# A causal mask as a product on TensorE in place of two selections on GpSimd: a macaron decoder layer with stick-breaking attention

## The chip, the cores and the metric

The kernel runs on one core of one Trainium2 chip. The metric is device microseconds (us) of one execution. The engines are TensorE (PE, with its weight loads PEld shown apart), VectorE (DVE), ScalarE (ACT), GpSimd (POOL) and SyncE (SP), which issues the transfers. Each runs its own list of instructions in order and they meet through semaphores.

## What is computed

One decoder layer on 1024 tokens of width 1024, all in float32: a SwiGLU block of inner width 2816, then a mixer block, then a second SwiGLU block, with RMS norms before each and at the end. The mixer has a pooling branch, an attention branch with 8 heads of 64, and gates. The attention branch is where the change lies. For query t and key s it computes

```python
z = (q . k) * scale
mask = kpos < qpos                                    # strictly causal
log_1m_beta = where(mask, log_sigmoid(-z), 0.0)
log_a = log_sigmoid(z) + reverse_cumsum(log_1m_beta) - log_1m_beta
a = where(mask, exp(log_a), 0.0)
out = a @ v
```

So a weight is sigmoid(z) times the product of 1 - sigmoid(z) over the keys between s and t. Where the mask is false the factor 1 - sigmoid is 1 and the weight is 0.

## The kernel before

Every float32 product is made of three products of fp32r operands (high by high, low by high, high by low), where fp32r is the type that the operands of these products have. All engines have lists written out by hand. The program runs through: norm and first SwiGLU, the combined input projection, the pooling branch, then the attention stage, the branch and output projections, the second SwiGLU and the last norm.

The attention stage works on 64 tiles, 8 heads by 8 query tiles of 128 rows; `TILE_ORDER` takes the query tiles of a head as 7, 6, 1, 0, 5, 4, 3, 2. A tile with query tile qt has (qt + 1) * 128 keys; up to 512 keys are one chunk, more are two, and the chunk that holds the diagonal comes first. There are 96 chunks. For each tile:

- PE, `logits`: q by k_hi, then q by k_lo, into one of three PSUM banks (L1334, L1336).
- ACT, `betas`: two sigmoids of the bank, 1 - beta into `keep` (L1811) and beta into `a` or `a2` (L1812); the second raises `sg_ok`.
- POOL, `mask_diagonal`: two `affine_select` on the last 128 columns of the tile, 1 into `keep` and 0 into `a` above the diagonal (L2626); each raises `masked`.
- DVE, `weigh_keys`: waits for `sg_ok` and `masked`, then a reversed scan of products over `keep` into `tail_p` (L2471), and `a` times `tail_p` (L2475, raises `a_ok`).
- PE, `turn`, two steps later: transposes the weights block by block with the identity `ident` (L1349).
- ACT, `turned_hi` (L1826), and DVE, `turned_lo` (L2484, raises `alo`): the high and low parts of what was turned.
- PE, `weigh`, once for two tiles: values by the turned weights (L1365 with the high part, L1366 with the low part).

Between these, PE runs the gates' products (L1188, `gate_parts`), 512 columns wide, in portions that `GATE_MARKS` sets for each step. They are independent of the attention and are there to fill the time in which PE would wait for a tile. After the stage the last gate products run (`GATE_TAIL`), then the branch projection (L1257).

POOL has little else in this stage: 16 products of a gate with the pooled branch (L2633).

At the program's start, POOL writes constants and the identity (L2610), and ACT, DVE and PE take the first norm, transposes and the first unit of the first SwiGLU (`up_units(0)`: a SiLU on ACT at L1496, then sums and low parts on DVE at L1905 and L1950 to L1999, then products on PE at L1047 and L1091).

Of the kernel before, what the change touches and what calls it, by code (L numbers as in the profile page):

```python
# [6 lines left out]
P = 128  # L7
# [96 lines left out]
TILES = attention_tiles()  # L104
NA = len(TILES)


CHUNKS = [sum(len(x["chunks"]) for x in TILES[:n]) for n in range(NA + 1)]
# [30 lines left out]
GATE_FIRST = [min(fb for fb, x in enumerate(GATE_BANKS) if x[0] == j) for j in range(KT)]  # L139
GATE_LAST = [max(fb for fb, x in enumerate(GATE_BANKS) if x[0] == j) for j in range(KT)]  # L140
PIECES = 4


def piece_start(j):
# [19 lines left out]
def macaron_layer(nc, x, ffn1_norm, ffn1_w_gate_up, ffn1_w_down, mix_norm, w_in, pool_w_group, pool_scale,  # L164
                  w_branch_pool, w_branch_attn, w_out, ffn2_norm, ffn2_w_gate_up, ffn2_w_down, final_norm, out):
    f32, f32r, i32 = mybir.dt.float32, mybir.dt.float32r, mybir.dt.int32
    ACT = mybir.ActivationFunctionType
    ALU = mybir.AluOpType
# [3 lines left out]
    with ctx:  # L172

        base = (nc.sbuf_base + 31) // 32 * 32
        K = 1024
# [5 lines left out]
        C0 = base + 200 * K  # L181
        G0 = C0 + 3200

        def at(name, shape, dt, offset):
            return nc.alloc_sbuf_tensor_at(name, shape, dt, offset=offset)
# [37 lines left out]
        for o0 in (120, 150):  # L223
            w = len(dn_slots)
# [58 lines left out]
        w_raw = at("w_raw", [P, 2, 2, KT, P], f32, R0)  # L283

        ident = at("ident", [P, P], f32, C0)
        o = C0 + 2560
        pos_i = at("pos_i", [P, PAD], i32, o)
        pos_f = at("pos_f", [P, PAD], f32, o + 64)
# [16 lines left out]
        zeros_f = at("zeros_f", [P, P], f32, base + 194 * K)  # L305
# [21 lines left out]
        keep = at("keep", [P, 2, SEQ], f32, X0 + 16384)  # L327
        a = at("a", [P, 2, SEQ], f32, X0 + 24576)
        a2 = at("a2", [P, SEQ], f32, o + 36864)
# [35 lines left out]
        def sem(name):  # L365
            return ctx.enter_context(nc.semaphore(name))
# [96 lines left out]
        gate_free = [sem(f"gate_free{b}") for b in range(2)]  # L463
        z_ok = sem("z_ok")
        sg_ok = sem("sg_ok")
        masked = sem("masked")
        scan_ok = sem("scan_ok")
        a_ok = sem("a_ok")
        t_ok = sem("t_ok")
# [534 lines left out]
        def _(pe):  # L1004
# [317 lines left out]
            def logits(n, part):  # L1322

                x_ = TILES[n]
                slot, qs = x_["head"] % 2, slice(x_["qt"] * P, (x_["qt"] + 1) * P)
                c, (c0, c1) = CHUNKS[n] + part, x_["chunks"][part]
                if n % NT == 0 and part == 0:
                    pe.wait_ge(head_in[slot], 96 * (x_["head"] // 2 + 1))
                if c in (0, 1):
                    wait_bank(2 + c, Q_GATE)  # L1330
                if c >= 3:
                    pe.wait_ge(sg_ok, c - 2)
                b, w = 2 + c % 3, c1 - c0
                nc.tensor.matmul(bank[:, b, 0:w], q_st[:, slot, qs], k_hi2[:, slot, c0:c1], start=True, stop=False,  # L1334
                                 skip_group_check=True)
                last = nc.tensor.matmul(bank[:, b, 0:w], q_st[:, slot, qs], k_lo2[:, slot, c0:c1], start=False,  # L1336
                                        stop=True, skip_group_check=True)
                last.then_inc(z_ok, 1)
# [33 lines left out]
            for s in range(NA + DRAIN):  # L1372
# [10 lines left out]
                if s < NA:  # L1383
                    n = len(TILES[s]["chunks"])
# [33 lines left out]
        def _(act):  # L1418
# [142 lines left out]
            def up_units(which):  # L1561

                even, odd, units = which, 1 - which, UNITS // 2 * which
                if which:
                    for i in range(2):
                        act.wait_ge(act_sp[i], 16 * units)
                plain_silu(which, 0, 0)
                plain_hi(which, 1, odd, units + 1)
                sums_of_u_hi(which, 0)
                sums_of_u_hi(which, 1)  # L1570
                plain_silu(which, 0, 1)
                sums_of_u_hi(which, 2)
                weights_hi(which, 2, even, units + 2)
                sums_of_u_hi(which, 3)
                sums_hi(which, 2, even)
                plain_silu(which, 1, 0)
                plain_silu(which, 1, 1)
                with act.Fori(1, UNITS // 2 - 1) as i:
                    up_unit(which, 2 * i, 0, units + i, more=(odd, units + i + 1))
                    up_unit(which, 2 * i + 1, 1, units + i, more=(even, units + i + 2))  # L1580
                n = UNITS - 2
                up_unit(which, n, 0, units + n // 2, more=(odd, units + n // 2 + 1))
                first_part(which, n + 1, 1, units + n // 2)
                dn_hi_of(2 * which, 0)
                silu(which, n + 1, 1, 0)
                second_part(which, n + 1, 1)
                dn_hi_of(2 * which, 1)
                silu(which, n + 1, 1, 1)
# [71 lines left out]
            def split_static(gg):  # L1660
                split_hi(gg, gg % 2, None if gg < 2 else quad_of(gg - 2))

            up_units(0)
            down(0, 2)

# [233 lines left out]
        def _(dve):  # L1899
# [564 lines left out]
            def weigh_keys(n):  # L2464

                w = TILES[n]["width"]
                dve.wait_ge(sg_ok, CHUNKS[n + 1])
                dve.wait_ge(masked, 2 * n + 2)
                if n:
                    dve.wait_ge(a_ok, n)  # L2470
                nc.vector.tensor_tensor_scan(tail_p[:, 0:w][:, ::-1], keep[:, n % 2, 0:w][:, ::-1],  # L2471
                                             zero_col[:, :].to_broadcast([P, w]), 1.0, ALU.mult, ALU.add).then_inc(scan_ok, 1)
                dve.wait_ge(scan_ok, n + 1)
                b = weights_of(n)[:, 0:w - 1]
                nc.vector.tensor_tensor(b, b, tail_p[:, 1:w], ALU.mult).then_inc(a_ok, 1)  # L2475
# [109 lines left out]
        @block.gpsimd  # L2585
        def _(pool):
            def norm_rows(k):

                for pos in range(NT):
                    t, n = pos, NT * k + pos  # L2590
                    pool.wait_ge(ms_ok, n + 1)
                    if k == 3 and t >= 4:
                        pool.wait_ge(part_ok, t - 3)
                        nc.gpsimd.tensor_scalar(mean_eps[:, k, t:t + 1], mean_sq[:, k, t:t + 1], part_sq[:, t:t + 1], EPS,
                                                ALU.add, ALU.add).then_inc(eps_ok, 1)
                    else:
                        nc.gpsimd.tensor_scalar(mean_eps[:, k, t:t + 1], mean_sq[:, k, t:t + 1], EPS, None,
                                                ALU.add).then_inc(eps_ok, 1)
                    pool.wait_ge(eps_ok, n + 1)
                    if n == 0:  # L2600
                        pool.wait_ge(half_set, 1)
                    nc.gpsimd.tensor_tensor(rstd[:, k, t:t + 1], mean_eps[:, k, t:t + 1], minus_half[:, :],
                                            ALU.pow).then_inc(rstd_ok, 1)

            nc.gpsimd.iota(pos_i[:, :], pattern=[[1, PAD]], base=1, channel_multiplier=0).then_inc(pos_set, 1)
            nc.gpsimd.memset(minus_half[:, :], -0.5).then_inc(half_set, 1)
            nc.gpsimd.memset(zeros_f[:, :], 0.0).then_inc(const_set, 1)
            nc.gpsimd.memset(zero_col[:, :], 0.0).then_inc(const_set, 1)
            pool.wait_ge(const_set, 2)
            nc.gpsimd.affine_select(out=ident[:, :], in_=zeros_f[:, :], compare_op=ALU.not_equal, fill=1.0, base=0,  # L2610
                                    pattern=[[-1, P]], channel_multiplier=1).then_inc(const_set, 1)
            norm_rows(0)
            norm_rows(1)

            pool.wait_ge(dn_ok, TAKEN)
            nc.gpsimd.memset(xpad[:, :, 0:PAD], 0.0).then_inc(const_set, 1)

            def weights_of(n):
                return a2[:, :] if n % 3 == 2 else a[:, n % 3, :]

            def mask_diagonal(n):

                w = TILES[n]["width"]
                pool.wait_ge(sg_ok, CHUNKS[n] + 1)
                for dst, fill in ((keep[:, n % 2, w - P:w], 1.0), (weights_of(n)[:, w - P:w], 0.0)):
                    nc.gpsimd.affine_select(out=dst, in_=dst, compare_op=ALU.is_gt, fill=fill, base=0,  # L2626
                                            pattern=[[-1, P]], channel_multiplier=1).then_inc(masked, 1)

            def gate_pool(i):

                pool.wait_ge(y_in[i % 2], 16 * (i // 2 + 1))
                pool.wait_ge(gate_free[0], i + 1)
                nc.gpsimd.tensor_tensor(gst[:, 0, :], gst[:, 0, :], pool_y[:, i % 2, :], ALU.mult).then_inc(gated, 1)  # L2633

            for s in range(NA + DRAIN):
                if s < NA:
                    mask_diagonal(s)
                for fb in BANKS_DONE[s]:
                    if fb % 2 == 0:
                        gate_pool(fb // 2)  # L2640
            norm_rows(2)
            norm_rows(3)
# [26 lines left out]
```

## Time and profile before

| | |
|---|---|
| median of 3 runs | 1937.92 us (1937.5 to 1938.38) |
| span of the profiled execution | 1937.1 us |
| PE busy | 1923.7 us, 99% |
| DVE / ACT / POOL busy | 69% / 40% / 7% |
| attention stage, 883 to 1156 us | 273.0 us, PE busy 270.76 |

The profile is of one execution; its span lies 0.8 us under the median of the runs, which is what the runs count around the span. Durations below are from that execution. A matmul's printed duration runs from its start to its modelled end, so it is longer than the distance to the next one: the distance of two starts is what a matmul costs PE.

### The profile page before, as it was taken

The numbers are of one execution on the slowest core, as the hardware profiler recorded it, in microseconds if no ns is written. First come the engines' busy times: TensorE is split into PE (matmuls) and PEld (weight loads), VectorE is DVE, ScalarE is ACT, GpSimd is POOL, SyncE is SP. The second block draws the span as 40 slices with busy tenths as digits, with TensorE's granted clock in tenths as the row PEclk, the third lists the DMA queues.
The fourth block names the chain that finished last, engine by engine and source line by source line (L and its number), as shares of the span: only waits on it lengthen the run. The fifth ranks groups of instructions, "written<-read, shape, count | busy, mean of one in ns | idle before, by whom it ended". The sixth has DMA issues, their size and how long they took to land.

```text
span 1937.1 us, 25171 instructions
## 1 busy us (share of the span) xinstructions
PE 1923.7 (99%) x9094; PEld 1607.4 (83%) x9094; DVE 1338.3 (69%) x1656; ACT 772.0 (40%) x1154; POOL 136.9 (7%) x218
## 2 busy tenths in 40 slices
PE   9999999999999999999999999999999999999998
PEld 9888888888888888888888888888888888888887
DVE  6987777775566667425777778789767776755655
ACT  7423232333434424214565652464323232324344
POOL 1000000000000100002333320010000000000002
PEclk9999999999999999999999999999999999999999
DMA  5456645468676503546645347643535454677665
GB/s 163 148 202 229 226 160 164 171 219 309 201 237 194 179 24 103 177 152 190 164 131 161 108 148 249 206 143 109 183 132 187 149 184 139 221 262 241 206 192 204
DMA packets 245092, 347.20 MB, mean 179 GB/s; under 512 B 16144, under 2 KB 150032, under 8 KB 240400
## 3 DMA queue, kind: packets, MB, share of 16 engines
q1 hardware_dynamic: 245008, 346.09, 54.9%
q8 instruction: 51, 0.84, 0.2%
q14 instruction: 33, 0.27, 0.0%
HBM read 232.79 MB, written 112.98 MB: 178 GB/s over the span
## 4 chain that ended last, share of the span: by engine, by line
PE 55%; DVE 2%; DMA 1%; issue 1%; ACT 1%; SPq 0%; POOL 0%; POOLq 0%; DVEq 0%; ACTq 0%
PE bank L1091 20%; PE bank L1188 12%; PE bank L1135 4%; PE bank L1137 4%; PE bank L1136 4%; PE bank L1047 2%; PE bank L1257 2%; PE bank L1285 2%; PE bank L1349 2%; DMA dn_lo_raw<-act_dram 1%; PE bank L1366 1%; PE bank L1365 1%; PE bank L1336 1%; PE bank L1334 1%; DVE tail_p L2471 0%
## 5 line engine op out<-in xcount | busy, mean ns | idle before, releaser
L1905 DVE TENSOR_TENSOR dn_lo<-dn_lo_raw,dn_hi 128x1024 fp32r<-128x1024 f32 x149 | 181.8, 1224 | 151.6 <-ACT dn_hi L1545 151.2
L1091 PE MATMUL bank<-hi_t,wa_hi 128*128 128x512 f32 x640 | 249.1, 389 | 0.2 <-issue 0.2
L1091 PE MATMUL bank<-hi_t,wa_lo 128*128 128x512 f32 x640 | 249.0, 389 | 0.0
L1091 PE MATMUL bank<-lo_t,wa_hi 128*128 128x512 f32 x640 | 249.0, 389 | 0.0
L1545 ACT ACTIVATE dn_hi<-dn_lo_raw 128x1024 fp32r<-128x1024 f32 x149 | 158.0, 1061 | 217.6 <-DMA dn_lo_raw<-act_dram 217.6
L1135 PE MATMUL bank<-dn_hi 128*128 128x512 f32 x596 | 232.7, 390 | 0.6 <-DVE dn_lo L1905 0.6
L1136 PE MATMUL bank<-dn_hi,dn_lo 128*128 128x512 f32 x596 | 231.9, 389 | 0.0
L1137 PE MATMUL bank<-dn_lo,dn_hi 128*128 128x512 f32 x596 | 231.9, 389 | 0.0
L1091 PE MATMUL bank<-hi_b,wa_hi 128*128 128x512 f32 x480 | 186.9, 389 | 0.5 <-DVE up L2029 0.5
L1091 PE MATMUL bank<-lo_b,wa_hi 128*128 128x512 f32 x480 | 186.8, 389 | 0.0
L1091 PE MATMUL bank<-hi_b,wa_lo 128*128 128x512 f32 x480 | 186.7, 389 | 0.0
L1905 DVE TENSOR_TENSOR wa_lo<-wa_lo_raw,wa_hi 128x1024 fp32r<-128x1024 f32 x132 | 174.3, 1350 | 5.6 <-ACT wa_hi L1485 0.5
L1188 PE MATMUL bank<-u_hi,w_hi 128*128 128x512 f32 x448 | 175.5, 392 | 0.0
L1188 PE MATMUL bank<-u_hi,w_lo 128*128 128x512 f32 x448 | 175.2, 391 | 0.0
L1188 PE MATMUL bank<-u_lo,w_hi 128*128 128x512 f32 x448 | 175.1, 391 | 0.0
L1525 ACT ACTIVATE g<-g 128x512 f32<-128x512 f32 x80 | 50.1, 627 | 263.9 <-DVE g L2037 257.7
L1091 PEld LDWEIGHTS bank<-hi_t,wa_hi 128*128 128x128 f32 x640 | 120.1, 188 | 25.4 <-issue 0.6
L1091 PEld LDWEIGHTS bank<-hi_t,wa_lo 128*128 128x128 f32 x640 | 120.1, 188 | 25.1
L1091 PEld LDWEIGHTS bank<-lo_t,wa_hi 128*128 128x128 f32 x640 | 120.1, 188 | 24.9
L1135 PEld LDWEIGHTS bank<-dn_hi 128*128 128x128 f32 x596 | 111.9, 188 | 24.6 <-DVE dn_lo L1905 1.7
L1137 PEld LDWEIGHTS bank<-dn_lo,dn_hi 128*128 128x128 f32 x596 | 111.9, 188 | 23.3
L1136 PEld LDWEIGHTS bank<-dn_hi,dn_lo 128*128 128x128 f32 x596 | 111.9, 188 | 23.2
(237 smaller groups left out, 3555.3 us busy)
## 6 DMA issues: line engine op xcount, KB each, us to landing
wa_lo_raw<-in_ffn_w_gate_up_dram SPq DMA_DIRECT2D x87, 512.0 KB, 5.0
dn_lo_raw<-act_dram SPq DMA_DIRECT2D x149, 256.0 KB, 4.3
act_dram<-g SPq DMA_DIRECT2D x44, 512.0 KB, 4.5
wd_t<-in_ffn_w_down_dram SPq DMA_DIRECT2D x44, 512.0 KB, 6.6
act_dram<-s_of SPq DMA_DIRECT2D x88, 256.0 KB, 6.5
wd_dram<-wd_t SPq DMA_DIRECT2D x22, 1024.0 KB, 6.0
dn_lo_raw<-wd_dram SPq DMA_DIRECT2D x85, 256.0 KB, 3.3
dn_lo_raw<-in_ffn_w_down_dram SPq DMA_DIRECT2D x64, 256.0 KB, 3.0
```

The source lines that it names most:

```text
L1047: last = nc.tensor.matmul(dst[:, cols], lhs, rhs, start=n == 0, stop=n == 3 * KT - 1, skip_group_check=True)
L1091: last = nc.tensor.matmul(acc, lhs, rhs, start=n == 0 and i != 2 and i < 5, stop=n == 11, skip_group_check=True)
L1135: nc.tensor.matmul(dst, a_hi_[:, toks], w_hi_, start=kf == 0 and DOWN[i][2], stop=False, skip_group_check=True)
L1136: nc.tensor.matmul(dst, a_lo_[:, toks], w_hi_, start=False, stop=False, skip_group_check=True)
L1137: end = nc.tensor.matmul(dst, a_hi_[:, toks], w_lo_, start=False, stop=last, skip_group_check=True)
L1188: last = nc.tensor.matmul(dst, lhs, (rhs_lo if p == 1 else rhs_hi)(kt), start=m == 0, stop=m == 3 * KT - 1)
L1257: last = nc.tensor.matmul(bank[:, b, :], weights(w_lo if p == 2 else w_hi, kt), (rhs_lo if p == 1 else rhs_hi)(kt), start=n == 0, stop=n = ...
L1285: last = nc.tensor.matmul(bank[:, 4 * s + place, :], pool_block(w_lo if p == 2 else w_hi, par, slot)[:, kt, :], rhs, start=n == 0 and i != ...
L1349: last = nc.tensor.transpose(bank[:, 5 + tb % 2, (kb % 4) * P:(kb % 4 + 1) * P], weights_of(n)[:, kb * P:(kb + 1) * P], ident[:, :])
L1525: nc.scalar.activation(g[s][:, half, :], g[s][:, half, :], ACT.Silu).then_inc(silu_ok, 1)
L1545: nc.scalar.activation(hi, raw, ACT.Copy).then_inc(dn_hi_ok, 1)
L1905: return nc.vector.tensor_tensor(dst, raw, hi.bitcast(f32), ALU.subtract)
```

## The change

Two constants are made at the program's start: `mask_f` on POOL by an `affine_select` (0 below the diagonal, -2^30 on it and above), and on ACT the copies `mask_r` and `ident_r` of the mask and of the identity in fp32r. In `logits`, in the chunk with the diagonal, a third matmul (identity by mask, 128 columns) is added between the two that were there, into the last 128 columns of the chunk. The sigmoids then give 1 and 0 by themselves. `mask_diagonal` on POOL goes, and with it the wait for `masked` in `weigh_keys`.

```diff
@@ logits
                 nc.tensor.matmul(bank[:, b, 0:w], q_st[:, slot, qs], k_hi2[:, slot, c0:c1], start=True, stop=False,
                                  skip_group_check=True)
+                if part == 0:
+                    if n == 0:
+                        pe.wait_ge(mask_set, 3)
+                    nc.tensor.matmul(bank[:, b, w - P:w], ident_r[:, :], mask_r[:, :], start=False, stop=False,
+                                     skip_group_check=True)
                 last = nc.tensor.matmul(bank[:, b, 0:w], q_st[:, slot, qs], k_lo2[:, slot, c0:c1], start=False,
@@ ACT, before up_units(0)
+            act.wait_ge(mask_set, 1)
+            nc.scalar.activation(mask_r[:, :], mask_f[:, :], ACT.Copy).then_inc(mask_set, 1)
+            nc.scalar.activation(ident_r[:, :], ident[:, :], ACT.Copy).then_inc(mask_set, 1)
             up_units(0)
@@ weigh_keys
                 dve.wait_ge(sg_ok, CHUNKS[n + 1])
-                dve.wait_ge(masked, 2 * n + 2)
@@ POOL, start
+            nc.gpsimd.affine_select(out=mask_f[:, :], in_=zeros_f[:, :], compare_op=ALU.is_gt, fill=MASK, base=0,
+                                    pattern=[[-1, P]], channel_multiplier=1).then_inc(mask_set, 1)
             norm_rows(0)
@@ POOL, attention stage
-            def mask_diagonal(n):
-
-                w = TILES[n]["width"]
-                pool.wait_ge(sg_ok, CHUNKS[n] + 1)
-                for dst, fill in ((keep[:, n % 2, w - P:w], 1.0), (weights_of(n)[:, w - P:w], 0.0)):
-                    nc.gpsimd.affine_select(out=dst, in_=dst, compare_op=ALU.is_gt, fill=fill, base=0,
-                                            pattern=[[-1, P]], channel_multiplier=1).then_inc(masked, 1)
             for s in range(NA + DRAIN):
-                if s < NA:
-                    mask_diagonal(s)
```

On PE, at the fourth tile (query tile 0, one chunk of 128 keys), the list before reads as follows; `ident,a` are the transposes of an earlier tile, `u_hi,w_lo` and its like the gates' products.

```order
L1188 MATMUL bank<-u_lo,w_hi 128x512
L1349 MATMUL bank<-ident,a 128x128 x7
L1334 MATMUL bank<-k_hi_214,q_st 128x128
L1336 MATMUL bank<-k_lo_215,q_st 128x128
L1188 MATMUL bank<-u_hi,w_lo 128x512
```

And with the change:

```order
L1192 MATMUL bank<-u_lo,w_hi 128x512
L1358 MATMUL bank<-ident,a 128x128 x7
L1338 MATMUL bank<-k_hi_217,q_st 128x128
L1343 MATMUL bank<-mask_r,ident_r 128x128
L1345 MATMUL bank<-k_lo_218,q_st 128x128
L1192 MATMUL bank<-u_hi,w_lo 128x512
```

One matmul is put in; nothing else on PE moves. The same holds for each of the 64 tiles.

On ACT, at the end of the first transposes, the list before:

```order
L1457 ACTIVATE hi_b<-bank 128x4x128
L1469 ACTIVATE lo_t_raw<-bank 128x512 x4
L1496 ACT_TABLE_LOAD
L1496 ACTIVATE g_69<-bank 128x512
L1485 ACTIVATE wa_hi_64<-wa_lo_raw 128x1024
```

And with the change:

```order
L1466 ACTIVATE hi_b<-bank 128x4x128
L1478 ACTIVATE lo_t_raw<-bank 128x512 x4
L1673 ACTIVATE mask_r<-mask_f 128x128
L1674 ACTIVATE ident_r<-ident 128x128
L1505 ACT_TABLE_LOAD
L1505 ACTIVATE g_69<-bank 128x512
```

The two copies stand ahead of the load of the SiLU's table and of the first SiLU.

## Rows read from the trace of the kernel before

**Rows 1.** Page, parts 1 and 2: busy time; TensorE's granted clock by slice.
```profile
PE 1923.7 (99%) x9094; PEld 1607.4 (83%) x9094; DVE 1338.3 (69%) x1656; ACT 772.0 (40%) x1154; POOL 136.9 (7%) x218
...
PEclk9999999999999999999999999999999999999999
```

**Rows 2.** Busy time by stretch, the attention stage: stretch, length, then each engine's busy us.
```profile
883.00:1156.00 273.00, 270.76 (x1522) 232.02 (x1521) 209.99 (x255) 162.26 (x381) 97.10 (x143) 1.00 0.52 149
```

**Rows 3.** Chain that ended last, behind the stage: start us, us, what.
```profile
1155.23 11.42 PE bank L1188 x50
1166.65 32.65 PE bank L1257 x144
```

**Rows 4.** Timeline, PE with a full weight buffer: start us, us, engine, line, operation.
```profile
1001.10 0.22 PE L1365 MATMUL bank<-at_hi,v_w 128*128 128x128 f32 x1
1001.10 0.19 PEld L1366 LDWEIGHTS bank<-at_lo,v_w 128*128 128x128 f32 x1
1001.16 0.28 PE L1366 MATMUL bank<-at_lo,v_w 128*128 128x128 f32 x1
1001.23 0.20 PEld L1349 LDWEIGHTS bank<-ident,a 128*128 128x128 f32 x2
```

**Rows 5.** Timeline, PE: two matmuls of 128 columns between wider ones.
```profile
1154.89 0.22 PE L1365 MATMUL bank<-at_hi,v_w 128*128 128x128 f32 x1
1154.95 0.28 PE L1366 MATMUL bank<-at_lo,v_w 128*128 128x128 f32 x1
1155.07 0.45 PE L1188 MATMUL bank<-u_lo,w_hi 128*128 128x512 f32 x1
1155.35 0.39 PE L1188 MATMUL bank<-u_hi,w_lo 128*128 128x512 f32 x1
1155.58 0.39 PE L1188 MATMUL bank<-u_hi,w_hi 128*128 128x512 f32 x1
```

**Rows 6.** Timeline, start of the program: ACT, DVE and PE around the first SiLU.
```profile
36.80 1.28 ACT L1496 ACT_TABLE_LOAD   x1
38.10 0.60 ACT L1496 ACTIVATE g<-bank 128x512 f32<-128x512 f32 x1
38.73 0.69 DVE L1986 TENSOR_TENSOR g<-g,bank 128x512 f32<-128x512 f32 x1 [3.07 <-ACT g L1496]
...
67.52 2.29 DVE L1905 TENSOR_TENSOR wa_lo<-wa_lo_raw,wa_hi 128x2048 fp32r<-128x2048 f32 x1
69.29 0.39 PE L1091 MATMUL bank<-hi_b,wa_lo 128*128 128x512 f32 x1
69.91 0.47 PE L1091 MATMUL bank<-hi_t,wa_hi 128*128 128x512 f32 x1 [0.23 <-issue]
```

**Rows 7.** Timeline, ACT: two operations of 128 columns in a row.
```profile
1004.62 0.28 ACT L1811 ACTIVATE keep<-bank 128x128 f32<-128x128 f32 x1
1004.79 0.27 ACT L1812 ACTIVATE a<-bank 128x128 f32<-128x128 f32 x1
```

**Rows 8.** Timeline, PE: the six waits of the stage.
```profile
897.58 1.05 PE L1349 MATMUL bank<-ident,a 128*128 128x128 f32 x7 [0.39 <-DVE at_lo L2484]
1025.97 0.39 PE L1365 MATMUL bank<-at_hi,v_w 128*128 128x256 f32 x1 [0.90 <-DVE at_lo L2484]
1042.60 0.88 PE L1349 MATMUL bank<-ident,a 128*128 128x128 f32 x6 [0.19 <-DVE a L2475]
1064.71 1.05 PE L1349 MATMUL bank<-ident,a 128*128 128x128 f32 x7 [0.24 <-DVE at_lo L2484]
1152.29 0.55 PE L1349 MATMUL bank<-ident,a 128*128 128x128 f32 x3 [0.22 <-DVE a L2475]
1154.08 0.39 PE L1365 MATMUL bank<-at_hi,v_w 128*128 128x256 f32 x1 [0.31 <-DVE at_lo L2484]
```

**Rows 9.** Waits of the stage: who waited for whom, us, times, longest.
```profile
DVE tail_p L2471 <- POOL a L2626: 2.4, 10, 0.2
```

**Rows 10.** Groups of POOL's instructions by line: busy us, mean ns.
```profile
L2626 POOL TENSOR_SCALAR_AFFINE_SELECT keep<-keep 128x128 f32<-128x128 f32 x64 | 42.1, 658 | 385.2 <-ACT a L1812 385.2
L2626 POOL TENSOR_SCALAR_AFFINE_SELECT a<-a 128x128 f32<-128x128 f32 x64 | 38.3, 598 | 0.0
```

More of the change, by code:

```diff
@@ L141 @@
 PIECES = 4
+MASK = -2.0 ** 30
 def piece_start(j):
@@ L285, in macaron_layer @@
         ident = at("ident", [P, P], f32, C0)
+        ident_r = at("ident_r", [P, P], f32r, C0 + 512)
+        mask_r = at("mask_r", [P, P], f32r, C0 + 1536)
+        mask_f = at("mask_f", [P, P], f32, base + 195 * K)
         o = C0 + 2560
@@ L465, in macaron_layer @@
         sg_ok = sem("sg_ok")
-        masked = sem("masked")
+        mask_set = sem("mask_set")
         scan_ok = sem("scan_ok")
@@ L2616, in _ @@
             nc.gpsimd.memset(xpad[:, :, 0:PAD], 0.0).then_inc(const_set, 1)
-            def weights_of(n):
-                return a2[:, :] if n % 3 == 2 else a[:, n % 3, :]
-            def mask_diagonal(n):
-                w = TILES[n]["width"]
-                pool.wait_ge(sg_ok, CHUNKS[n] + 1)
-                for dst, fill in ((keep[:, n % 2, w - P:w], 1.0), (weights_of(n)[:, w - P:w], 0.0)):
-                    nc.gpsimd.affine_select(out=dst, in_=dst, compare_op=ALU.is_gt, fill=fill, base=0,
-                                            pattern=[[-1, P]], channel_multiplier=1).then_inc(masked, 1)
             def gate_pool(i):
```

## The prediction, made before the changed kernel ran

> **What bounds the kernel now.** I read the page's busy times first. PE is busy 1923.7 of 1937.1 us and its clock stands at the full level in every slice [rows 1], so 13.4 us in all is the most that any removed wait could give back. Next come the stretches: in the attention stage, the only one the change touches besides the start, PE is busy 270.76 of 273.00 us, DVE 209.99, ACT 162.26 and POOL 97.10 [rows 2]. Then the chain that ended last: behind the stage it runs on PE without a break, from the gates' products into the branch projection [rows 3], so what the stage grows by is passed on to the end in full. Work put on PE here is paid; work taken from POOL is repaid only where PE now waits for what POOL holds up.
>
> **The added product.** It is 64 matmuls of 128 columns, one for each tile. The question is what one costs PE. The rows give two answers. By columns alone it is small: a matmul of 128 columns and the next start 0.06 us apart (1001.10 and 1001.16, 1154.89 and 1154.95) [rows 4, 5]. But every matmul here has its own weight load, and the loads show the other answer. The load for L1366 starts at 1001.10, when the matmul ahead of it starts, and the next load starts only at 1001.23 [rows 4]: one load is held back until the weights before it are in use, and takes about 0.11 to 0.13 us. The two narrow matmuls are paid behind: the 512-wide matmul after them lasts 0.28 us to the next start (1155.07 to 1155.35) where the one after takes 0.23 (1155.35 to 1155.58) [rows 5]. From 1154.89 to 1155.35 is 0.46 us; less 0.23 for the wide one leaves 0.23 for two, that is 0.115 us each. I take this value, since the added matmul stands in the same place: between two matmuls with weights of their own, the identity ahead of q again. Its own load hides under q by k_hi, but the load of q for k_lo can start only when the mask's matmul does, and nothing but 128 columns covers it. So 64 x 0.115 = **7.4 us**. The ends are 64 x 0.06 = 3.8 us (columns alone, if the reload of q is hidden) and 64 x 0.13 = 8.3 us (the distance of the two loads).
>
> The Trainium skill, page "TensorE: Matmul & The Clock Gate", section "Back-to-back issue gap", gives a sustained spacing of about 81 ns for pairs of load and matmul with 128 columns; by that the term would be 64 x 0.081 = 5.2 us and the sum 4.5, an estimate from the page. The rows here show 115 ns for this pair, and the measurement decides.
>
> **The two copies on ACT at the start.** They stand ahead of the SiLU's table load at 36.80 and the first SiLU at 38.10 [rows 6]. DVE has been idle for 3.07 us when that SiLU releases it at 38.73 [rows 6], so ACT is what is late there. Two operations of 128 columns start 0.17 us apart on ACT (1004.62 and 1004.79) [rows 7], so two copies push the SiLU back by 0.34 us. From 38.73 DVE has work without pauses worth the name until the low parts at 67.52 to 69.81, and PE, which starts a matmul at 69.29 and could start the next 0.23 us later, starts it at 69.91 [rows 6]. The profile names "issue" there, but DVE's end at 69.81 is 0.1 us ahead and that product waits for it. PE has no slack at this place, so I count **+0.34 us** in full. The ends: 0 if ACT's delay is caught up by DVE's short gaps, 0.56 if each copy costs its printed 0.28.
>
> **The constants on POOL.** One selection of 128 columns is put between the identity and the first norm's work. POOL waits there for the first transfers anyway; the mask is needed by ACT after 36 us and by PE after 883 us. The wait on PE ahead of the first mask is long met and queues nothing. Cost 0.
>
> **What goes from POOL.** 128 selections, 42.1 + 38.3 = 80.4 us of POOL [rows 10]. It is an engine that is mostly idle, so this is no gain in itself. DVE waited for it 10 times, 2.4 us in all, 0.24 each [rows 9]. PE does not wait for POOL anywhere in the stage. PE waits for DVE in six places, with 0.39, 0.90, 0.19, 0.24, 0.22 and 0.31 us idle [rows 8], 2.25 together, which is the 273.00 - 270.76 of the stretch [rows 2]. These count from the modelled end of the matmul before, 0.39 us behind its start, where the next could start after 0.23; so each loses some 0.16 more, and the six lose 2.25 + 6 x 0.16 = 3.2 us. That is the bound of what the removed selections can give.
>
> What of it is given back: the wait at 1152.29 is behind a scan that waited 0.24 us for the last selection, so I count 0.24. In the first four places the work of a gate product with the pooled branch on POOL, a transfer, or DVE's own queue is what was late, and that stays. But there PE itself comes later: a mask or two (three at 897.58, where three tiles have gone by) lies between the work that the late chain starts from and the wait, and takes the place of idle time. That is 3 x 0.11 at 897.58, and about 0.11 to 0.15 at each of the other three, 0.7 together. The wait at 1154.08 starts from PE's own transposes with no mask between and stays. Sum **-1.0 us**, between 0 and -3.2.
>
> **The sum.** 7.4 + 0.34 + 0 - 1.0 = +6.7 us on the span: 1937.1 + 6.7 = 1943.8 for a profiled span, and with the 0.8 us around it 1937.92 + 6.7 = **1944.6 us** for the median, 0.35% slower. ScalarE's sigmoids see each chunk about 0.1 us later, and DVE gets rid of a wait of twice that size where it had one; neither is a new bound, since DVE is busy for 77% and ACT for 59% of the stage [rows 2].
>
> **The rivals.**
> *The reload of q is hidden (not slower by what can be told).* If PE takes the load of q for k_lo while q by k_hi still runs, a mask costs its columns, 0.06 us [rows 4, 5]. Against it speak rows 4, where a load starts with the matmul ahead and never before; for it, that q_st is read twice running and that no row shows an identity in fp32r. Then 3.8 + 0.34 - 1.0 = +3.1: 1941.1 us, and 1939.0 if all 3.2 us of waits go. It decides at 0.075 us for one mask: below it the total is under 3.9 us.
> *The removed selections free DVE (faster).* GpSimd's selections run long beside DVE's work, 658 and 598 ns in the mean [rows 10], so the two engines may hold each other up. If all of PE's 3.2 us of waits are owed to that, they go, and even with the cheapest mask the sum is 3.8 + 0.34 - 3.2 = +0.9: 1938.9. It would be faster only with a mask under 0.045 us, which no row has. The Trainium skill, "GPSIMD Engine Reference", section "8. Key points", says that GpSimd shares its SBUF interfaces with VectorE and contends with instructions with two SBUF inputs; the long selections agree with it, but it changes no chance here, as the waits bound the gain.
> *Each mask costs more, or the later logits open a new wait.* At 0.14 us for one and no wait absorbed it is 9.0 + 0.56 = +9.5: 1947.4. PE would have to wait for ACT or DVE anew at many tiles; the fill of gate products speaks against it.
>
> **How the numbers follow.** This kernel's measurement can tell about 0.2%, 3.9 us, from no change. The forecast, a mask of 0.10 to 0.13 us, gives 5.7 to 7.8 us: chance 0.69. The hidden reload, with part of the cases between, gives 1 to 4 us: 0.20, of which nearly all lies within 0.2%. More than 8.3 us: 0.08. Faster than before by over 0.2%: 0.03, for something that no row shows. The range takes in the forecast and half of the cheaper case: 1940.8 to 1946.6. Faster 0.03, same 0.19, slower 0.78.
>
> **What would show it.** In the changed trace, by the distance of starts: from q by k_hi to q by k_lo in a 512-wide chunk, 0.34 us instead of 0.23 where no transposes lie ahead, and most of it on the row of q by k_lo or the one ahead of it. The attention stage grows by some 6.4 us, the stretch ahead of it by 0.34, first seen at the matmul after 69.29; everything behind only shifts. DVE's waits for POOL are gone, and the stage's idle time on PE falls from 2.25 us to 1.3 to 1.6. Wrong it would be if the stage grows by under 4 us (reload hidden) or if idle time on PE rises (a new wait).

## The result and the profile after

The changed kernel takes 1944.59 us (median of 6 runs, 1944.21 to 1945.04), the kernel before 1938.15 (6 runs, 1937.37 to 1938.56). The ratio is 1.0034 with a 95% interval of 1.0023 to 1.0046: 6.4 us slower. The forecast was 1944.6 us, 6.7 more than the 1937.92 known then.

The page's busy times and the granted clock, answering to [rows 1]:

```profile
PE 1931.2 (99%) x9158; PEld 1615.9 (83%) x9158; DVE 1337.7 (69%) x1656; ACT 775.7 (40%) x1156; POOL 59.8 (3%) x91
...
PEclk9999999999999999999999999999999999999999
```

PE has 64 instructions more and 7.5 us more of busy time at an unchanged clock; POOL has lost 77.1 us, and the kernel is not the faster for it.

The attention stage as a stretch, in the columns of [rows 2]:

```profile
884.00:1162.00 278.00, 276.38 (x1581) 238.79 (x1579) 207.86 (x254) 164.83 (x379) 19.91 (x15) 1.00 0.51 145
```

It starts 0.7 us later and PE is idle for 1.62 us in it instead of 2.24. Measured by starts, from the first q by k_hi to the last values product, the stage took 271.57 us (883.38 to 1154.95) and now takes 277.90 (884.08 to 1161.98): +6.33.

One chunk of 512 keys shows the price. Timeline of PE and its weight loads, the kernel before:

```profile
909.47 0.47 PE L1334 MATMUL bank<-k_hi,q_st 128*128 128x512 f32 x1
909.55 0.19 PEld L1336 LDWEIGHTS bank<-k_lo,q_st 128*128 128x128 f32 x1
909.78 0.39 PE L1336 MATMUL bank<-k_lo,q_st 128*128 128x512 f32 x1
909.78 0.19 PEld L1188 LDWEIGHTS bank<-u_hi,w_lo 128*128 128x128 f32 x1
910.01 0.40 PE L1188 MATMUL bank<-u_hi,w_lo 128*128 128x512 f32 x1
910.24 0.40 PE L1188 MATMUL bank<-u_hi,w_hi 128*128 128x512 f32 x1
```

The same chunk with the change:

```profile
910.65 0.47 PE L1338 MATMUL bank<-k_hi,q_st 128*128 128x512 f32 x1
910.73 0.19 PEld L1343 LDWEIGHTS bank<-mask_r,ident_r 128*128 128x128 f32 x1
910.96 0.22 PE L1343 MATMUL bank<-mask_r,ident_r 128*128 128x128 f32 x1
910.97 0.19 PEld L1345 LDWEIGHTS bank<-k_lo,q_st 128*128 128x128 f32 x1
911.02 0.45 PE L1345 MATMUL bank<-k_lo,q_st 128*128 128x512 f32 x1
911.07 0.19 PEld L1192 LDWEIGHTS bank<-u_hi,w_lo 128*128 128x128 f32 x1
911.31 0.40 PE L1192 MATMUL bank<-u_hi,w_lo 128*128 128x512 f32 x1
911.55 0.39 PE L1192 MATMUL bank<-u_hi,w_hi 128*128 128x512 f32 x1
```

The mask's own load (910.73) starts 0.23 us ahead of its matmul and costs nothing. The load of q for k_lo starts at 910.97, with the mask's matmul, and the load after it only at 911.07. The mask's row to the next row is 0.06 us, and the other 0.06 sits on the row of q by k_lo, which lasts 0.29 to the next start instead of 0.23. In this chunk, reading one row's distance alone gives half the price. From q by k_hi to the second gate product it is 0.90 instead of 0.77.

Over all tiles that follow transposes, that distance (from q by k_hi to the second row behind q by k_lo) is, in the mean:

| keys in the diagonal chunk | before, us | after, us | more, us |
|---|---|---|---|
| 128 (16 tiles) | 0.539 | 0.652 | 0.113 |
| 256 (16) | 0.555 | 0.665 | 0.110 |
| 384 (15) | 0.663 | 0.777 | 0.114 |
| 512 (15) | 0.775 | 0.899 | 0.124 |

The mean is 0.115, times 64 is 7.4 us: the term of the forecast.

### The profile page after: what moved, and what is told of

Same layout as the page of the kernel before. It is cut to its first block, busy times and chain, and to the rows that moved or that the text cites. A ratio compares the mean times of both kernels' runs of the same rounds, so it can differ in the third digit from the quotient of the medians.

```text
span 1943.2 us, 25110 instructions
## 1 busy us (share of the span) xinstructions
PE 1931.2 (99%) x9158; PEld 1615.9 (83%) x9158; DVE 1337.7 (69%) x1656; ACT 775.7 (40%) x1156; POOL 59.8 (3%) x91
## 4 chain that ended last, share of the span: by engine, by line
PE 59%; DVE 1%; issue 0%; ACT 0%; POOLq 0%; POOL 0%; DVEq 0%; ACTq 0%
PE bank L1095 20%; PE bank L1192 13%; PE bank L1139 5%; PE bank L1140 5%; PE bank L1141 5%; PE bank L1051 2%; PE bank L1261 2%; PE bank L1289 2%; PE bank L1358 2%; PE bank L1345 1%; PE bank L1375 1%; PE bank L1374 1%; PE bank L1338 1%; PE bank L1026 0%; DVE tail_p L2482 0%
```

## The experiments

The stage in the table is the distance of starts used above; sums is the start of the first product of hi_t, the place that the forecast named for the delay of the start. All times are medians, with the ratio to the kernel before in the same job.

| kernel | us | ratio (95%) | stage, us | sums, us |
|---|---|---|---|---|
| before | 1938.15 | | 271.57 | 69.91 |
| changed | 1944.59 | 1.0034 (1.0023 to 1.0046) | 277.90 | 70.21 |
| no product | 1938.34 | 1.0001 (0.9991 to 1.0010) | 271.36 | 70.23 |
| both masks | 1944.48 | 1.0032 (1.0021 to 1.0044) | 277.66 | 70.25 |
| product twice | 1950.93 | 1.0067 (1.0049 to 1.0085) | 283.96 | 70.04 |
| product of 256 columns | 1944.59 | 1.0034 (1.0021 to 1.0047) | 277.66 | 70.41 |
| late copies | 1944.24 | 1.0033 (1.0021 to 1.0045) | 277.89 | 69.87 |
| selections gone | 1937.91 | 0.9999 (0.9990 to 1.0008) | 271.26 | 69.86 |
| gate products on VectorE | 1937.32 | 0.9995 (0.9986 to 1.0004) | 270.68 | 69.78 |

**The product taken out again.**

```diff
-                if part == 0:
-                    if n == 0:
-                        pe.wait_ge(mask_set, 3)
-                    nc.tensor.matmul(bank[:, b, w - P:w], ident_r[:, :], mask_r[:, :], ...)
```

> The changed kernel without its 64 mask products (its attention weights above the diagonal are therefore not masked: that part of the result is left out); the constants and ScalarE's two copies at the start stay, GpSimd's selections stay away. Theory (the products are the whole loss, 7.4 us, and removing the selections gives little): 0.3 us for the copies, less about 0.2 for the last wait of the stage, so 1938.2 us (1937.6 to 1938.7), and the attention stage as long as before, 271.3 to 271.6 us from the first q by k_hi to the last values product. Rival (the selections held VectorE up and their removal frees TensorE, which the products then overpay): 3 us under the kernel before, 1935.3.

Measured 1938.34 us, stage 271.36. The products are the loss; what is left, selections gone and two copies added, can't be told from the kernel before. PE's waits in the stage did not go with the selections: PE was busy 269.87 of 272.00 us, so it was idle for 2.13, before for 2.24.

```profile
883.00:1155.00 272.00, 269.87 (x1519) 231.57 (x1517) 207.22 (x254) 161.87 (x379) 19.94 (x15) 1.00 0.52 149
```

**The selections put back beside the product.**

```diff
+                dve.wait_ge(masked, 2 * n + 2)
...
+                if s < NA:
+                    mask_diagonal(s)
```

> The changed kernel with GpSimd's 128 selections and VectorE's wait for them put back, so that both masks are applied. Theory: the selections cost TensorE next to nothing, 1944.6 to 1945.2 us, the one wait of 0.24 us near the stage's end back. Rival (the selections' removal repaid a part of the products): up to 3 us over the changed kernel, 1947.6.

Measured 1944.48 us, no different from the changed kernel, and 0.1 under the range. DVE's ten waits are back, as in [rows 9]:

```profile
DVE tail_p L2484 <- POOL a L2641: 2.4, 10, 0.2
```

The wait of PE near the stage's end came back in part: 0.16 us idle at 1158.63, where the changed kernel has 0.02 at 1159.32. The expected 0.24 us more did not come all the same; the stage is even 0.24 shorter. The experiment that takes nothing but the selections out says why.

**The product issued twice.**

```diff
                     nc.tensor.matmul(bank[:, b, w - P:w], ident_r[:, :], mask_r[:, :], ...)
+                    nc.tensor.matmul(bank[:, b, w - P:w], ident_r[:, :], mask_r[:, :], ...)
```

> The changed kernel with each mask product issued twice (64 more of 128 columns). Theory (a narrow product costs the weight load that it can't cover, 0.115 us): 64 x 0.115 = 7.4 more, less some 0.3 taken out of waits, so 1951.7 us (1951.0 to 1952.2). Rival (a product costs its columns, 0.06 us, and the first one paid something once, such as the exchange of q's weights): 3.8 more, 1948.4.

Measured 1950.93 us, 6.3 more than the changed kernel, and 0.1 under the range that the theory gave; 2.5 over the rival. The second product costs what the first did. Timeline of PE, a chunk of 512 keys:

```profile
910.46 0.47 PE L1338 MATMUL bank<-k_hi,q_st 128*128 128x512 f32 x1
910.77 0.22 PE L1343 MATMUL bank<-mask_r,ident_r 128*128 128x128 f32 x1
910.83 0.27 PE L1345 MATMUL bank<-mask_r,ident_r 128*128 128x128 f32 x1
910.94 0.45 PE L1347 MATMUL bank<-k_lo,q_st 128*128 128x512 f32 x1
911.22 0.40 PE L1192 MATMUL bank<-u_hi,w_lo 128*128 128x512 f32 x1
```

The second mask starts 0.06 us behind the first and q by k_lo 0.11 behind the second. By the distance used in the table of chunks it adds 0.108, that is 6.9 us for 64. The stage grew by 6.06, so more of it went into PE's waits than the 0.3 us that I had put down.

**The product made 256 columns wide.**

```diff
-                    nc.tensor.matmul(bank[:, b, w - P:w], ident_r[:, :], mask_r[:, :], ...)
+                    m = min(2 * P, w)
+                    nc.tensor.matmul(bank[:, b, w - m:w], ident_r[:, :], mask_r[:, 2 * P - m:], ...)
...
+            (on ScalarE, a copy of zeros into the first 128 columns of mask_r)
```

> The changed kernel with the mask product 256 columns wide in the 48 tiles whose diagonal chunk has 256 keys or more (128 zero columns ahead of the mask; one more copy on ScalarE at the start). Theory (the load of the next weights, about 0.115 us, sets the price, and 256 columns take 0.114): no more than 0.3 us, with 0.15 of it at the start, so 1944.5 to 1945.0 us. Rival (columns set the price): 48 x 0.057 = 2.7 us more, 1947.3.

Measured 1944.59 us, the same as with 128 columns, against 1947.3 by the rival. This is the run that settles that it is not columns that are paid for. Timeline of PE and of two of its weight loads, the same chunk:

```profile
910.32 0.47 PE L1338 MATMUL bank<-k_hi,q_st 128*128 128x512 f32 x1
910.64 0.28 PE L1344 MATMUL bank<-mask_r,ident_r 128*128 128x256 f32 x1
910.64 0.19 PEld L1346 LDWEIGHTS bank<-k_lo,q_st 128*128 128x128 f32 x1
910.75 0.40 PE L1346 MATMUL bank<-k_lo,q_st 128*128 128x512 f32 x1
910.76 0.19 PEld L1192 LDWEIGHTS bank<-u_hi,w_lo 128*128 128x128 f32 x1
910.99 0.39 PE L1192 MATMUL bank<-u_hi,w_lo 128*128 128x512 f32 x1
```

Now the mask's row lasts 0.11 us and q by k_lo 0.24: the sum from 910.64 to 910.99 is the 0.35 that it is with 128 columns (910.96 to 911.31). Over the 46 wider chunks of the table the distance grew by 0.004 us, where the rival had 0.057. That the time is that of the next load is read from the load rows: the load of q for k_lo starts with the mask, and the one behind it 0.10 us later with 128 columns (910.97 to 911.07) and 0.12 with 256 (910.64 to 910.76). Every matmul of this program has a load of its own (9158 of each in the changed kernel), so no run parts the load from another fixed cost of that size for a pair of load and matmul.

**The copies moved away from the start.**

```diff
-            act.wait_ge(mask_set, 1)                      # ahead of up_units(0)
-            nc.scalar.activation(mask_r[:, :], mask_f[:, :], ACT.Copy).then_inc(mask_set, 1)
-            nc.scalar.activation(ident_r[:, :], ident[:, :], ACT.Copy).then_inc(mask_set, 1)
...
+            (the same three lines)                        # ahead of take_pool(0)
```

> The changed kernel with ScalarE's two copies of the constants moved from ahead of the first SiLU to the start of the mixer block, ahead of the pooling rows (the mask's source gets a place of its own). Theory (the copies delay the first SiLU by 0.3 us and TensorE has no slack behind it): 0.3 us under the changed kernel, 1944.3 us, and the first product of the sums at 69.9 us instead of 70.2. Rival (the shift at the start is caught up later): no change, 1944.6.

Measured 1944.24 us. The difference of 0.35 from the changed kernel has the expected sign and size but is within what the runs scatter; the trace is what shows it. The changed kernel's start, in the order ACT, DVE, PE:

```profile
36.58 0.31 ACT L1673 ACTIVATE mask_r<-mask_f 128x128 fp32r<-128x128 f32 x1
36.77 0.31 ACT L1674 ACTIVATE ident_r<-ident 128x128 fp32r<-128x128 f32 x1
37.10 1.28 ACT L1505 ACT_TABLE_LOAD   x1
38.40 0.60 ACT L1505 ACTIVATE g<-bank 128x512 f32<-128x512 f32 x1
39.03 0.69 DVE L1998 TENSOR_TENSOR g<-g,bank 128x512 f32<-128x512 f32 x1 [3.46 <-ACT g L1505]
...
42.45 0.19 PEld L1051 LDWEIGHTS bank<-hi_b,wa_hi 128*128 128x128 f32 x1 [0.31 <-DVE wa_lo L1917]
42.46 0.50 PE L1051 MATMUL bank<-hi_b,wa_hi 128*128 128x512 f32 x1
```

And with the copies moved:

```profile
36.77 1.28 ACT L1505 ACT_TABLE_LOAD   x1
38.06 0.60 ACT L1505 ACTIVATE g<-bank 128x512 f32<-128x512 f32 x1
38.69 0.69 DVE L1998 TENSOR_TENSOR g<-g,bank 128x512 f32<-128x512 f32 x1 [3.06 <-ACT g L1505]
```

Against [rows 6] the first SiLU starts 0.30 us later in the changed kernel (38.40, before 38.10) and at its old place here (38.06). The sums start at 70.21 and 69.87. Over all the kernels of the table with the two copies at the start they start at 70.04 to 70.25, and without copies there at 69.78 to 69.91.

**Nothing but the selections taken out of the kernel before.**

```diff
-                dve.wait_ge(masked, 2 * n + 2)
...
-                if s < NA:
-                    mask_diagonal(s)
```

> The kernel before without GpSimd's 128 selections and VectorE's wait for them, nothing in their place and no constants (the causal mask on the diagonal blocks is left out). Theory: 0 to 0.5 us under the kernel before, 1937.9 us, with VectorE's ten waits for GpSimd gone and TensorE's waits for VectorE nearly all still there. Rival (the two engines hold each other up): 3 us under it, 1935.

Measured 1937.91 us, no change. The rival of freed engines falls: 77 us of POOL's work gave nothing that the time shows, and DVE's busy time fell only from 1338.3 to 1336.8 us, so the selections had hardly held DVE up. PE's waits, counted by starts (what a wait adds to the distance of two starts), sum to 3.2 us, before to 3.3, but they are not the same ones. One is new, at 984. Timeline of the kernel before there:

```profile
982.16 0.69 DVE L2475 TENSOR_TENSOR a<-a,tail_p 128x511 f32<-128x511 f32 x1
982.17 0.84 POOL L2626 TENSOR_SCALAR_AFFINE_SELECT a<-a 128x128 f32<-128x128 f32 x1
982.98 1.72 POOL L2633 TENSOR_TENSOR gst<-gst,pool_y 128x512 f32<-128x512 f32 x1
983.47 2.04 DVE L2471 TENSOR_TENSOR_SCAN tail_p<-keep,zero_col 128x384 f32<-128x384 f32 x1
```

And with the selections gone:

```profile
981.79 1.57 POOL L2632 TENSOR_TENSOR gst<-gst,pool_y 128x512 f32<-128x512 f32 x1 [17.57 <-ACT gst L1854]
982.31 1.60 DVE L2474 TENSOR_TENSOR a<-a,tail_p 128x511 f32<-128x511 f32 x1
983.97 0.66 PE L1349 MATMUL bank<-ident,a 128*128 128x128 f32 x4 [0.30 <-DVE a L2474]
```

POOL's product of a gate with the pooled branch holds DVE up. In this trace's stage and in that of the kernel before, 11 DVE operations each on tiles in SBUF alone (products of weights, scans, low parts of the gates' weights) start while such a product runs. Each of them ends behind the product by its own usual length less 0.13 to 0.15 us, as if it had stood still until then: here the product ends at 983.36, and DVE's operation of usually 0.69 us at 983.91. Operations that had started ahead of the product are longer by at most 0.09, and those that read a PSUM bank are as short as ever. It goes the other way too, and that is where the selections' long durations in [rows 10] come from: 73 of the 128 take 0.33 us at most, and each of the other 55 ends 0.09 to 0.16 us behind a scan or a product of DVE beside which it ran. Timeline of the kernel before:

```profile
1038.64 1.30 POOL L2633 TENSOR_TENSOR gst<-gst,pool_y 128x512 f32<-128x512 f32 x1 [0.98 <-ACT gst L1854]
1038.99 0.29 DVE L2484 TENSOR_TENSOR at_lo<-bank,at_hi 128x128 fp32r<-128x128 f32 x1 [2.12 <-ACT at_hi L1826]
1039.20 2.35 DVE L2471 TENSOR_TENSOR_SCAN tail_p<-keep,zero_col 128x768 f32<-128x768 f32 x1
1039.89 1.76 POOL L2626 TENSOR_SCALAR_AFFINE_SELECT keep<-keep 128x128 f32<-128x128 f32 x1
```

The low part from the bank takes 0.29 us in the midst of the product; the scan takes 2.35 instead of the 1.75 that scans of its width have elsewhere, and the selection beside it 1.76 instead of 0.29.

Before, at 982, two selections stood ahead of the product on POOL and it met a scan that nobody waited for (2.04 us instead of 0.96). With POOL empty it starts 1.2 us sooner and meets the product of the weights (1.60 instead of 0.69), which PE's transposes wait for. Two of PE's six waits became shorter or vanished (0.07 us idle for 0.22 at 1152, none at 1064), and this one took their place. The changed kernel has it too, at 987.01, and the kernel with both masks has not, which fits its stage being 0.24 us shorter.

**The gate products moved to VectorE.**

```diff
-                        gate_pool(fb // 2)                # on GpSimd, at step s
+                        gate_pool(fb // 2)                # on VectorE, at step s + 1
...
```

> The kernel before, its selections on GpSimd kept, with the 16 products of a gate with the pooled branch moved from GpSimd to VectorE, one step later in VectorE's list. In the traces these products overlap with VectorE's work and stretch it (a low part of 0.69 us takes 1.45 to 1.73, a scan of 0.95 takes 2.04), ahead of three of TensorE's six waits in the stage. Theory (these collisions make a part of the 3.2 us of waits): VectorE gets 16 x 0.69 = 11 us of work and loses about as much of stretching; TensorE's waits fall by 0.5 to 1.8 us, so 1936.3 to 1937.6 us. Rival (VectorE's own queue makes the waits, and more work there only adds to them): no change or up to 2 us more, 1938 to 1940.

Measured 1937.32 us over 11 runs, ratio 0.9995 (0.9986 to 1.0004): in the range of the theory, but not told apart from no change by its own runs. The stage is 0.9 us shorter, 270.68. DVE's low parts of the gates' weights are short again, 707 ns in the mean instead of 877 (columns as in [rows 10]), at the price of 10.5 us of new work for the 15 products that lie in the stage:

```profile
L2496 DVE TENSOR_TENSOR w_lo<-w_raw,w_hi 128x512 fp32r<-128x512 f32 x28 | 19.7, 707 | 11.0 <-ACT w_hi L1847 11.0
L2505 DVE TENSOR_TENSOR gst<-gst,pool_y 128x512 f32<-128x512 f32 x15 | 10.5, 702 | 0.0
```

DVE's busy time is 1339.1 us, before 1338.3: the new work took almost only what DVE had lost standing still. Where PE waits shifted once more. If anything in this stage is to be gained, it is here and not in the mask, and by the stage of this one execution it is about 1 us.

## Why the prediction was right, step by step

**The bound.** PE was the limit and stayed it. What was put on PE came through almost whole; what was taken from POOL did not come back.

**The added product, 7.4 us.** Right in size and mechanism: 0.115 us for one, measured over the chunks. The choice between 0.06 and 0.115 was the step on which the forecast stood. Only the first is to be seen on the narrow matmul's own row; the second needs the rows behind it, as in [rows 5], and the loads, as in [rows 4]. The doubled product and the wide one bear it out. One sign that the forecast named was wrong as written: from q by k_hi to q by k_lo in a chunk of 512 without transposes ahead, 0.34 us. The one such chunk has 0.28 (884.08 to 884.37), 0.06 more than the 0.23 before, and by that alone one would have taken the rival of the hidden reload for true; the other 0.06 lie on the row of q by k_lo. The lower price that the Trainium skill gives ("TensorE: Matmul & The Clock Gate", "Back-to-back issue gap", about 81 ns) would have made 5.2 us of this term; the runs show 7.4.

**The copies, +0.34 us.** 0.30 measured, but the place was read wrongly. I had PE pay at 69.91. It paid at 42.46, where a wait of 0.31 us for DVE's low part of the weights appeared that the kernel before does not have. From there PE is late by as much as DVE, and its wait ahead of the sums is as long as before (0.22 us, before 0.23). I had looked only at waits that the old trace shows; here a matmul whose operand DVE had so far finished just in time was the first to be late.

**The constants on POOL, 0.** Right: the new selection takes 0.29 us, and POOL then still waits 3.65 us. It waits for ScalarE, not for the first transfers as I had it.

**The waits given back, -1.0 us.** The sum was right, its make-up only in part. The stage grew by 6.33 instead of 7.4, so 1.05 came back; PE's idle time fell to 1.62 us, at the edge of the 1.3 to 1.6 that I had named. Of the waits in [rows 8], the first went from 0.39 to 0.28 us idle (three masks, where I had counted 0.33 less), the second from 0.90 to 0.75, the third from 0.19 to 0.03 and the fifth, at 1152.29, from 0.22 to 0.02, near the 0.24 that I had counted; the last stayed at 0.31, as argued. The wait at 1064.71 vanished, which it also does with the selections alone taken out, and a new one of 0.22 appeared at 987.01:

```profile
987.01 0.33 PE L1358 MATMUL bank<-ident,a 128*128 128x128 f32 x1 [0.22 <-DVE a L2486]
1030.71 0.39 PE L1374 MATMUL bank<-at_hi,v_w 128*128 128x256 f32 x1 [0.75 <-DVE at_lo L2495]
1161.10 0.39 PE L1374 MATMUL bank<-at_hi,v_w 128*128 128x256 f32 x1 [0.31 <-DVE at_lo L2495]
```

By starts the larger waits sum to 2.7 us instead of 3.3, so they hold 0.6 of the 1.05; the rest is in gaps of under 0.13 us that I did not tell apart. The new wait I did not foresee: I had held that what was late in the first four places, the gate products on POOL among it, "stays", and those moved when the selections ahead of them went.

**The sum.** 0.30 + 6.33 = 6.6 us by the stages, 6.4 by the medians, 6.0 by the profiled spans (1943.2 and 1937.1, where the forecast had 1943.8). That the time agrees with the forecast to 0.1 us is luck beyond that: the kernel before came out at 1938.15 over six runs instead of 1937.92. The 0.8 us between span and median, too, were not what the runs count around the span. That is 1.7 to 2.1 us wherever a run has its own span on record (1944.93 and 1943.2 for the changed kernel's profiled run), so the profiled execution of the kernel before took about 1938.9 us, by an estimate from these, 0.7 over the median of 1938.15. The forecast of the median does not rest on it. Two things in the traces belong to neither kernel. The changed one waits 0.23 us for DVE at 634.79, and so does the kernel with gate products on VectorE, whose program up to there is that of before; the other kernels don't. The kernel before waits 0.55 at 1753.10, and no other kernel does; that is near the 0.7 us by which this execution lay over the median. Each profile is one execution, and waits of this size come and go in it.

```profile
634.79 0.33 PE L1026 MATMUL bank<-ident,u_lo_raw 128*128 128x128 f32 x1 [0.23 <-DVE h L2188]
```

```profile
1753.10 0.50 PE L1135 MATMUL bank<-dn_hi 128*128 128x512 f32 x1 [0.55 <-DVE dn_lo L1905]
```

The first of these is of the changed kernel, the second of the kernel before.

**The rivals.** The hidden reload is ruled out by the load of q for k_lo, which starts with the mask's matmul at 910.97 and not under q by k_hi, and by the 6.33 us of the stage, where it had under 4. Its point of decision was slightly off: a total of 3.9 us belongs to a mask of 0.071 us, not 0.075, and its 1939.0 is 1938.9 by its own sum. The freed VectorE is ruled out by the selections taken out alone. A new wait did open, but a single one, of 0.22 us idle, and the waits that went are more.

## What to carry to other kernels

A small product put between two others, each with weights of its own, cost 0.115 us here whether it had 128 columns or 256, which fits the weight load that it can't cover; add up the distance from the row ahead to the second row behind before you call it cheap. Work on an idle engine costs nothing until some engine waits for it, so before moving it onto the engine that is the bound, find a wait that goes with it. And when an engine is emptied, ask what else it runs: that may start sooner, and beside other work than before.

## What the runs showed that I had not expected

The delay at the start was paid at a matmul for which the old trace has no wait (42.46 us). And an engine's selections can be of use by standing in the way: with them gone, a product on GpSimd came 1.2 us sooner and held up a VectorE operation that TensorE waits for, 1.60 us instead of 0.69.
